# A two-block transformer kernel on one core: residual stream turned to features on partitions, side work spaced by a clock of TensorE time

## The reference, cut to what matters

```
layer A: x += concat(sigmoid(o) * rmsnorm(mlstm(q,k,v,i,f)) * silu(z), memory_attention) @ w_out   # h = rmsnorm(x)
shared:  k, v  = from rmsnorm(x) @ w_kv_a, a latent norm, @ w_kv_b, rmsnorm, rope
layer B: x += concat(chunk_causal_attention(q,k,v) * silu(z), memory_attention) @ w_out
block C: x += (concat(multiscale_pool(u), rms_norm(diff_attention(q,k,v))) * sigmoid(g)) @ w_out
block D: x += memory_cross_attention(rms_norm(x), rms_norm(mem_2)) @ w_co
block E: x += square(relu(rms_norm(x) @ w_up)) @ w_down          # 1024 -> 4096 -> 1024
return rms_norm(x)
```

## Time and profile before

| | |
|---|---|
| median of 3 runs | 1754.74 us (1748.2 to 1758.79) |
| profiled execution, its own time | 1747.94 us |
| span of its trace | 1746.0 us |
| PE matmul busy | 1629.9 us (93% of the span), 7336 records |
| PE weight load busy | 1269.4 us (73%) |
| DVE busy | 889.9 us (51%) |
| ACT busy | 753.1 us (43%) |
| POOL busy | 69.9 us (4%) |
| mean granted TensorE clock | 0.974 |

### The profile page before, as it was taken

One profiled execution on the slowest core, in us unless ns is written; L12 is line 12 of the kernel. 1 busy time (PEld: TensorE's weight loads), 2 busy tenths in 40 slices (PEclk: granted clock), 3 DMA queues, 4 the chain that ended last, 5 costly groups with the idle time before them and its releaser, 6 DMA issues.

```text
span 1746.0 us, 19776 instructions
## 1 busy us (share of the span) xinstructions
PE 1629.9 (93%) x7336; PEld 1269.4 (73%) x7336; DVE 889.9 (51%) x1879; ACT 753.1 (43%) x1714; POOL 69.9 (4%) x64
## 2 busy tenths in 40 slices
PE   6996999999999978899899999889999999999997
PEld 5574777777787866666678877467786878888886
DVE  4367446738445464555544647445444453434343
ACT  6353333324345556666433343335323443434342
POOL 0011001101000000000000000000000000000000
PEclk9998999999999999999999999689999999999999
DMA  6221222222333211111123222013232323333332
GB/s 202 72 82 37 73 61 73 84 62 86 132 103 115 67 38 50 45 46 47 61 74 108 85 73 85 1 50 108 86 108 79 103 85 98 97 100 95 98 98 78
DMA packets 85119, 141.54 MB, mean 81 GB/s; under 512 B 7200, under 2 KB 32160, under 8 KB 85024
## 3 DMA queue, kind: packets, MB, share of 16 engines
q1 hardware_dynamic: 83728, 137.45, 25.5%
q10 hardware_dynamic: 1296, 2.83, 0.5%
HBM read 138.17 MB, written 2.10 MB: 80 GB/s over the span
## 4 chain that ended last, share of the span: by engine, by line
PE 61%; DVE 13%; issue 13%; ACT 10%; DMA 1%; POOL 1%; ACTq 0%; DVEq 0%; SPq 0%; POOLq 0%
PE banks L1059 10%; PE banks L1061 10%; PE banks L1060 10%; PE banks L1054 7%; PE banks L1056 7%; PE banks L1055 7%; DVE sb_arena L1711 3%; ACT sb_junk L1318 3%; PE banks L1019 3%; DVE sb_arena L1720 2%; DVE sb_w_split L1711 2%; ACT sb_w_split L1355 2%; ACT sb_arena L1484 1%; PE banks L1243 1%; DVE sb_arena L1714 1%
## 5 line engine op out<-in xcount | busy, mean ns | idle before, releaser
L1711 DVE TENSOR_TENSOR sb_w_split<-sb_raw,sb_w_split 128x512 fp32r<-128x512 f32 (+4 forms) x520 | 322.6, 662 | 367.2 <-ACT sb_w_split L1355 366.3
L1355 ACT ACTIVATE sb_w_split<-sb_raw 128x512 fp32r<-128x512 f32 (+4 forms) x520 | 286.1, 600 | 352.7 <-PE banks L1061 193.3
L1059 PE MATMUL banks<-sb_w_split,sb_actB 128*128 128x512 f32 (+2 forms) x752 | 302.3, 402 | 7.2 <-DVE sb_w_split L1711 3.0
L1061 PE MATMUL banks<-sb_w_split,sb_actB 128*128 128x512 f32 (+2 forms) x752 | 291.5, 388 | 0.0
L1060 PE MATMUL banks<-sb_w_split,sb_actB 128*128 128x512 f32 (+2 forms) x752 | 291.2, 387 | 0.0
L1054 PE MATMUL banks<-sb_actA,sb_w_split 128*128 128x512 f32 x672 | 271.9, 405 | 1.6 <-DVE sb_arena L1720 1.5
L1056 PE MATMUL banks<-sb_actA,sb_w_split 128*128 128x512 f32 x672 | 262.9, 391 | 0.0
L1055 PE MATMUL banks<-sb_actA,sb_w_split 128*128 128x512 f32 x672 | 262.5, 391 | 0.0
L1059 PE MATMUL banks<-sb_w_split,sb_actA 128*128 128x512 f32 (+1 forms) x416 | 167.8, 403 | 2.2 <-DVE sb_arena L1720 2.2
L1059 PEld LDWEIGHTS banks<-sb_w_split,sb_actB 128*128 128x128 f32 x752 | 144.0, 192 | 32.9 <-DVE sb_w_split L1711 5.6
L1061 PEld LDWEIGHTS banks<-sb_w_split,sb_actB 128*128 128x128 f32 x752 | 143.1, 190 | 28.2
(11 more groups left out here) (163 smaller groups left out, 1864.1 us busy)
## 6 DMA issues: line engine op xcount, KB each, us to landing
sb_raw<-in_a_w_in SPq DMA_DIRECT2D x64, 256.0 KB, 3.0
sb_raw<-in_w_up SPq DMA_DIRECT2D x32, 512.0 KB, 3.6
sb_raw<-in_w_down SPq DMA_DIRECT2D x32, 512.0 KB, 3.7
sb_raw<-in_w_in SPq DMA_DIRECT2D x24, 512.0 KB, 3.6
sb_raw<-in_mem_w_kv SPq DMA_DIRECT2D x16, 512.0 KB, 3.8
sb_raw<-in_a_w_in SPq DMA_DIRECT2D x16, 512.0 KB, 3.7
sb_raw<-in_w_ckv SPq DMA_DIRECT2D x16, 512.0 KB, 3.7
sb_raw<-in_a_w_out SPq DMA_DIRECT2D x12, 512.0 KB, 3.7
```

The costliest lines, as they stand in the source:

```text
L1059: pe.op.matmul(out, x.hi(k)[:, cs], hi, start=i == 0, stop=False)
L1061: t = pe.op.matmul(out, x.lo(k)[:, cs], hi, start=False, stop=last_i)
L1355: act.op.activation(hi[:, cs], raw[:, cs], ACT.Copy).then_inc(act.mark(m("w_hi"), 2 * n + part + 1), 1)
L1711: dve.op.tensor_tensor(out, a, b, op).then_inc(dve.mark(*mark) if mark else dve.tick(), 1)
```

## The change

- **Residual by features.** `x`, `mem` and `mem_2` come in transposed and the result leaves transposed, on the host side of the kernel. `x_res` is [128, 8, 512]. `turn` has no transposes any more: ACT and DVE read `x_res` in SBUF. The products that end in the residual take the form "feature". Squares are written by ACT (`sqa`), added up by POOL (`sqp`), and summed over partitions by PE against a column of ones (`nsq`); the final norm is made in the same way and applied by DVE to eight feature tiles.
- **Planner.** A clock sums the PE time of what is placed (`row_ns`, `side_ns`). A group is taken when the clock has moved by the group's own distance (`lag`) since the last of its lane. `need` now forces only the lane that holds the step (`force`).
- **Layer B reordered**: qlB, ckvB, mk1, mv1, zB0, kvB0, quB0, mqB, kvB1, quB1, mzB0, mzB1 and so on; softmax groups of layer B turn a unit two groups after its scores, with three probability buffers. In D both key products come first, then both query products, then both value products.
- **Gates** by two `tensor_tensor_scan` instructions in place of the eighteen doubling steps.
- **Start**: x is loaded first in eight tiles and `mqA` is the first product, then the memory.

```
-            add(f"{name}{half}", w, nk * P, [(half * 512, 512)], "token", src, "res", order=order, k0=k0)
+            add(f"{name}{half}", w, nk * P, [(half * 512, 512)], "feature", src, "res", order=order, k0=k0)
...
     def advance(self, lane):
-        if self.lanes[lane] and all(a in self.done for a in self.lanes[lane][0][0]):
-            for step in self.lanes[lane].popleft()[1]:
-                self.put_side(lane, step)
+        if self.lanes[lane]:
+            after, steps, lag = self.lanes[lane][0]
+            if all(a in self.done for a in after) and self.clock - self.last[lane] >= lag:
+                self.take(lane)
...
+    def force(self, step):
+
+        if any(step in group for group in self.soon):
+            for s in self.soon.popleft():
+                self.put(s)
+            return
+        lane = next((n for n in (0, 1) if any(step in group[1] for group in self.lanes[n])), None)
+        missing = [a for a in self.lanes[lane][0][0] if a not in self.done]
+        if missing:
+            self.force(missing[0])
+        else:
+            self.take(lane)
...
     def need(self, *steps):
-        tries = 0
-        while not all(s in self.done for s in steps):
-            tries += 1
-            self.step()
+        for step in steps:
+            while step not in self.done:
+                self.force(step)
...
+    def mem_b(h0):
+        rounds(0, [("B", h, i) for h in (h0, h0 + 1) for i in range(TT)], "msc", "mtp", "mval",
+               [("hnscale", "mqB"), ("hnt", "mk1", 3)], [("silu", f"mzB{h0 // 2}", 1)], depth=2, lag=2400)
...
+    latents(0)
+    p.product("mqB")
+    mla(0)
+    head_norm(1, "mqB", TT, True)
+    mem_b(0)
+    mem_b(2)
+    latents(1)
+    p.need(("nrow", "b"))
+    gated("mzB0")
+    gated("mzB1")
+    mla(2)
+    latents(2)
+    p.need(("mval", "B", 3))
+    gated("zB1")
...
-        p.side(0, after, *group)
+        p.side(0, after, *group, lag=4600)
...
+    for kind in ("nsq", "nsum", "ndiag", "nrow"):
+        p.put_side(0, (kind, "f"))
+    for k in range(KD):
+        p.put(("store", k))
...
+            blocks = [(v.sq_sum[norm], 0)] if tiles == TT else [(v.sq_sum[norm], 0), (v.sq_sum[norm], N_MEM)]
+            if norm == "f":
+                blocks += [(v.square_of(norm, n)[1], 0) for n in range(4, KD)]
...
+            for i in range(tiles):
+                for n, (block, at) in enumerate(blocks):
+                    t = pe.op.matmul(v.ps[:, place.bank, i:i + 1], block[:, at + i * P:at + (i + 1) * P], v.con("ones"),
+                                     start=n == 0, stop=n == len(blocks) - 1)
...
         elif kind == "turn":
             name, k = a
-            _, tiles, gain, dst = v.turn(name)
-            second_part(step, dst, k, v.col(gain, k), n=tiles * P)
+            src, gain, dst = v.turn(name, k)
+            dve.wait_ge(*m.at("t_hi", step))
+            fused(dst.lo(k), src, gain, ALU.mult, dst.hi(k).bitcast(F32), ALU.subtract, *m.at("t_lo", step))
...
+            dve.op.tensor_tensor_scan(g[6], g[7], g[5], 0.0, ALU.mult, ALU.add).then_inc(dve.tick(), 1)
...
+            dve.op.tensor_tensor_scan(g[3], g[1], g[1], 0.0, ALU.max, ALU.max).then_inc(dve.tick(), 1)
...
+        elif kind == "sqp":
+            norm, n = a
+            signal, value = m.at("sq_sum", step)
+            pool.wait_ge(*m.at("sq", ("sqa", norm, n)))
+            if n >= 2:
+                pool.wait_ge(signal, value - 1)
+            total = v.sq_sum[norm]
+            pool.op.tensor_tensor(total, total, v.square_of(norm, n)[1], ALU.add).then_inc(signal, 1)
```

More of the change, by code:

```diff
@@ L278, in __init__ @@
         self.chunk_place = []
+        self.clock, self.last = 0.0, [0, 0]
+        self.ahead = 2
     def put(self, step, banks=()):
@@ L358, in product, with after_residual @@
                 self.step()
+    def after_residual(self, name):
+        norm, turn, first = NORM_AFTER[name[:-1]], TURN_AFTER.get(name[:-1]), 4 * int(name[-1])
+        for j in range(first, first + 4):
+            steps = [("turn", turn, j)] if turn else []
+            if first:
+                for step in steps:
+                    self.put(step)
+                self.soon.append(squares(norm, j))
+            else:
+                self.soon.append(steps + squares(norm, j))
     def finish(self):
@@ L371, in order_of_work, with turns, scales @@
     p = Plan()
[L373 to L379 removed]
+    def turns(name, tiles):
+        for k in tiles:
+            p.soon.append([("turn", name, k)])
+    def scales(lane, norm, row=True, after=(), lag=4000):
+        p.side(lane, after, lag=0)
+        p.side(lane, (), ("nsq", norm), ("nsum", norm), lag=lag)
         if row:
[L381 to L383 removed]
+            p.side(lane, (), ("ndiag", norm), ("nrow", norm), lag=4500)
     def head_norm(lane, x, n_tiles, in_softmax):
@@ L397, in head_norm, with rounds @@
                 p.side(lane, (), *steps)
[L399 to L403 removed]
+    def rounds(lane, units, scores, turn_over, values, after, values_after=(), depth=1, lag=4400):
+        complete, first = None, True
+        for n in range(len(units) + depth):
             group = []
@@ L407, in rounds @@
                 complete = None
-            if u is not None:
-                group.append((scores, *u))
-            if before is not None:
-                group.append((turn_over, *before))
-                if before[-1] == TT - 1:
-                    complete = before[:-1]
-            before = u
-            p.side(lane, after if first else values_after if group[0][0] == values else (), *group)
-            first = False
-        p.side(lane, values_after, (values, *complete))
-    turns(0, "memT", range(KD), squares=lambda n: [("sq", "mem", n // 2)] if n % 2 else [])
@@ L421, in order_of_work @@
-    p.side(0, (), ("masks",), ("nsum", "mem"))
-    turns(0, "hA", range(KD), [("load_x", TT - 1)], squares=lambda n: [("sq", "a", n)])
-    scales(0, "a")
-    p.need(("turn", "memT", 3))
-    p.soon.extend([(("load_x", i),) for i in range(2, TT)])
-    p.product("mk0", [("nsum", "mem")])
-    head_norm(1, "mk0", MT, False)
+            if n < len(units):
+                group.append((scores, *units[n]))
+            if n >= depth:
+                u = units[n - depth]
+                group.append((turn_over, *u))
+                if u[-1] == TT - 1:
+                    complete = u[:-1]
@@ new lines, in rounds @@
+            p.side(lane, after if first else values_after if group[0][0] == values else (), *group, lag=lag)
+            first = False
+        p.side(lane, values_after, (values, *complete), lag=1000)
+    for n in range(2):
+        p.put(("load_x", n))
+        p.put(("fetch", n))
+    p.n_fetch = 2
+    p.put(("load_x", 2))
+    p.put(("turn", "hA", 0))
+    p.put(("split", 0))
+    p.put(("fetch", 2))
+    p.put(("load_x", 3))
+    p.put(("turn", "hA", 1))
+    p.put(("split", 1))
+    p.n_split, p.n_fetch = 2, 3
@@ new lines, in order_of_work @@
+    for k in range(4, KD):
+        p.put(("load_x", k))
+        if k % 2:
+            p.put(("fetch", p.n_fetch)) if k == 5 else None
+    p.n_fetch = 4
+    for n in range(4):
+        p.put(("load_mem", n))
+    for k in range(KD):
+        p.soon.append(([("turn", "hA", k)] if k >= 2 else []) + squares("a", k))
+    for n in range(4):
+        p.soon.append([("turn", "memT", 2 * n), ("turn", "memT", 2 * n + 1)] + squares("mem", n))
+    p.soon.append([("masks",)])
+    scales(0, "a", after=[("sqp", "a", 7)], lag=0)
@@ L480, in order_of_work @@
     p.put(("load_again",))
-    turns(1, "memTb", range(KD))
     p.product("outA0")
-    turns(0, "hB", range(4))
+    p.put(("load_mem_again",))
     p.product("outA1")
     p.put(("enter", "outA1"))
-    turns(0, "hK", range(KD))
-    scales(0, "b")
+    turns("hK", range(KD))
+    scales(0, "b", after=[("sqp", "b", 7)])
+    for k in range(KD):
+        p.soon.append([("turn", "memTb", k)])
+    p.product("qlB", [("nsum", "b")])
+    for step in (("qll0",), ("qll1",)):
+        p.side(1, (), step, lag=1500)
```

604 lines of the change are left out of this document (309 added, 295 removed).

## The result

The changed kernel takes 1768.93 us (median of five runs, 1764.55 to 1770.57) beside 1754.74 for the kernel before in the same comparison; the ratio is 1.0078, with a 95% interval of 1.005 to 1.0106: small, but clear of no change. The prediction was 1684, with a range of 1642 to 1716. Its profiled execution has a span of 1768.8 us against 1746.0.

What follows compares the result with a forecast made beforehand. PE was taken as the bound, losing time to side work and waits for late inputs. Terms -27 + 6 - 10 - 22 - 25 - 1 + 0 + 3 + 9 = -67 gave 1684 us, range 1642 to 1716.

Steps and rivals of the forecast that it cites:

- I take 42.3 down to 17: Layer B: longer turn distances remove most waits, about 10 forced memory groups add 11 us back; -25, bounds 0 and -36.
- B not relieved: Rival: layer B's 25 us stays lost through forced groups before zB1 and busier ACT; 1709, chance 0.15.
- Gates: Layer A's gate stretch: scans replace doubling steps and memory softmaxes are no longer forced along; 27.5 to 6, -22 us.
- Both forms stand in that stretch at one pace: Feed-forward blocks: residual products changing from token to feature form keep the same matmul pace; 0 us.
- D: Layer D: m2's squares and additions before nrow m2 at ckD0 make an 8 us stall; 11.0 to 14, +3.
- Start and end: Start: -10, bounds -3 and -15; after the last product matmul: 19.0 us, +9, or +13 with ones at low clock.
- Transposes and ones: PE side matmuls: 240 transposes gone, -27 us; sums against ones for seven norms, +6 us.
- PE's total would be down by some 29: Sign to look for: PE's total busy time down by some 29, 240 transposes at modelled length plus less slow clock.
- C: Layer C: lane still blocked behind gC0, same sixteen softmaxes pile up at outC0; 39.6 stays, 0, bounds -12 and +5.
- The rival of POOL: POOL's 44 additions hold up DVE at each norm; +26 us, 1710, chance 0.06.
- The rival that the kernel gets slower: Distances too long, so needs force groups in bulk in A, B and D; more than 32 extra forced; chance 0.04.

Runs made afterwards that it cites:

- lag0: Kernel after, with the planner taking a group as soon as its conditions hold, whatever its distance: 1775.33 us, 1.0126 of before.
- memfirst: Kernel after, layer B reordered with ckvB first, mqB behind mk1, memory softmaxes before the first pair's attention, pair-turn distances halved: 1765.18 us.
- bonly: Kernel after, only layer B's order changed: mqB, ckvB, mk1, mv1, mzB0, qlB, mzB1, then pairs; pair and latent turn distances 1300: 1753.84 us.
- best3: Kernel after with near, gateblock, bonly's order, mem_2's squares placed in outC1, and dveadd together: 1699.31 us, 0.9706 of before.
- noconv: Kernel after, convolution of head 0 in layer A with two taps instead of four: 1756.49 us, 1.0033 of before.
- gatesfirst: Kernel after, gate matmul groups and the gates' first step put ahead of the norm of mk0 in lane 1: 1782.42 us, 1.0163 of before.
- near: Kernel after, tensor actB allocated right after actA instead of last in SBUF: 1755.58 us, 1.0013 of before.
- gateblock: Kernel after, in block C the group with a head's last dval waits for gC4's gates instead of gC0's: 1738.68 us, 0.9908 of before.
- dveadd: Kernel after, the 44 additions of squares made by DVE instead of POOL: 1761.48 us, 1.0044 of before.
- swap: Kernel after, actA and actB exchanged in the allocation, so actB is second and actA last: 1768.56 us (one run).

## Why the prediction was wrong

**The step that failed most: layer B, 48 us off.** The step was "I take 42.3 down to 17": turns two groups late, distances and two products of room were to take away nearly all of B's waits, and about 10 forced memory groups were to put 11 us back. The planner forces 13 groups, and that stretch loses 17.6: a forced softmax costs more than 2.0 less its own matmuls, because behind short waits the matmuls ran at the low clock. That is 7 of the 48. The rest is the relief that did not come: outside the forced stretch layer B still loses 63, where all of it lost 59.1 before. Forcing 7 groups and not 13 (lag0) changed nothing, so the number forced is not what makes the loss. What was missed is where the side work goes. The new order puts qlB, ckvB, mk1 and mv1 first and mqB eighth, so that the first 97 us (495.7 to 592.5) carry 5 us of side matmuls and all 66 softmax groups come later. I had counted groups against rows from mqB on and never asked what the kernel before did with the rows ahead of it: there mqB came third and the memory softmaxes ran beside ckvB and qlB. With the memory softmaxes early again, memfirst and bonly lose 65.0 and 63.9 instead of 80.8: some 16 of the 48 are the order, the forced stretch included. The other 30 are a relief that no order tried has brought; best3 ends at 59.3, level with the kernel before. The rival "B not relieved" (1709) was the right direction with a floor that was too kind: it let B be as before, not worse.

**Gates, 20 us off (17 with the rest of layer A).** Two assumptions failed. The forecast took all of the loss to be doubling steps and forced softmaxes. The scans alone, in the kernel before, bring 9.7 of 25.3; of the 15.6 that stay, the convolution's DVE work is the one part that a run shows, in the kernel after (noconv, 9.0). And "x first" was costed only at the start: behind it the memory's key norm stands ahead of the gates in their lane, so the gates' matmuls run in qkA0, up to 117.7, and their chain ends after the last row of it, where PE waits 3.27 us for the transposes. gatesfirst shows the price of that, 8.4 us in this stretch. Queue order after a moved load is a part of moving it.

**The operand's place, 11.5 us, absent from the sum.** "Both forms stand in that stretch at one pace" was true of the kernel before and useless, since both operands lay near the front. 144 rows of residual products at 0.08 us each are 11.5, and the 384 matmuls of the token products out of actB add 2.5; near measured 13.4. 5.1 of it (64 rows) more than explain the feed-forward blocks' +4.0, the rest is spread over the other parts of the table and is not to be added to them.

**D, 9 us too small.** The mechanism was right, a chain of squares and additions before `nrow m2` at the foreseen place; its size was not. I put four squares and three additions in it; POOL ran six additions, since those of the residual's own norm stand ahead. With 9.37, 1.81 and 1.03 us idle and the clock at half behind that, 8 us of stall became 17 of loss.

**Start and end.** The first product matmul came at 7.92 us (8.4 predicted). But the stages up to qkA0 lose 3.6 less, not 10, near the bound of 3, though not for its reason: the rows of mqA, now the first product, lose 7.7, and only 0.83 of that is a wait for a split. The longest is for the diagonal of x's own norm, which DVE makes behind evictions and turns of the memory:

```profile
38.03 2.05 PE L1246 MATMUL banks<-sb_arena 128*128 128x512 f32 x2 [3.53 <-DVE sb_arena L1865]
```

The rest is matmuls 0.43 us apart, at half pace, in the first 6 us. The forecast had no term for the norm's chain there. After the last product matmul 21.5 us pass for 19: the twenty ones-matmuls take 6.78 for 4.1, at the low clock, as the bracket of +13 had it.

```profile
1748.75 6.78 PE L1237 MATMUL banks<-sb_cons,sb_arena 128*128 128x1 f32 x40 [1.49 <-issue]
```

**What held.** Transposes and ones: -20.4 by price. That PE's total would be down by some 29 did not hold, since slow matmuls took its place. C: 0 predicted, +2.3; the block behind gC0 is unchanged, and gateblock shows that it is the dearest single line in the kernel after (it stands in the kernel before too, with a pile behind it as well, but was not lifted there). The rival of POOL: dveadd brings 7.4 us of the feared 26, 4.4 of them in D. Beside POOL's additions in D (from 1212.91 on) a pair of splits took 2.56 us, the pair before them 1.29:

```profile
1211.83 1.29 DVE L1862 TENSOR_TENSOR sb_w_split<-sb_raw,sb_w_split 128x512 fp32r<-128x512 f32 x2 [2.33 <-ACT sb_w_split L1505]
1213.90 2.56 DVE L1862 TENSOR_TENSOR sb_w_split<-sb_raw,sb_w_split 128x512 fp32r<-128x512 f32 x2 [0.79 <-ACT sb_w_split L1505]
```

The Trainium skill (SBUF — State Buffer, "SBUF: two separate sides") says that GpSimd and a DVE instruction with two SBUF inputs share a pair of ports, which one of them holds for its whole instruction while the other is blocked. The second row agrees that DVE is held up; the run shows that most of what is held up had slack.

**The forecast's shape.** The rival that the kernel gets slower had 0.04 and came true, but not by its mechanism, bulk forcing by distances: distances were a gain in A and nothing in B (lag0). Each large term was read as what an edit removes. Three of the misses are things that an edit moved: product rows to where no side work was ready, the gates behind another norm, a tensor to the end of memory.

What stays open: which move in layer B's order brings the 16 us, and the last 59 us of layer B, which neither order removes; DVE and ACT alternate there inside each softmax, and no run took that apart.

## What to carry to other kernels

Where one engine sets the pace and the rest is packed around it, an order of products is also a supply of cover: list, for each product, which side work is ready when it runs, before and after, and price the rows that run with none. A wait condition in a queue costs everything behind it; moving one condition in C from the last gate product to the one whose data it guards was worth more than the whole change was meant to bring in any one layer. And an edit of the memory layout is an edit of speed until a trace shows that it isn't.

## What the runs showed of the hardware

- A matmul of 512 columns in fp32r with an operand in the last tensor of SBUF (48 KB, from some 178,000 bytes of the partition on) starts 233.3 ns after the one before it, against 226.7 with the tensor near the front, at the same full clock. It follows the tensor in swap. It holds for the moving operand (dn, up) and for the stationary one (mv0 233.0 and 226.8, kC 233.4 and 228.0). Products out of the memory in the kernel before, whose tensor lies near the front, have 230 to 231, and no run takes that apart. Where between front and end the change comes was not tried.
- At equal work, 7194 matmul records, PE's busy time is 1649.4 us in the kernel after, 1629.5 with one wait condition moved (gateblock) and 1601.2 in best3, of which the place of the operand makes 12.4. In the forced stretch of layer B, waits of 0.4 to 1.5 us, each harmless by itself, are followed by a stretch at 1.2 GHz in which the same value step took 3.75 us instead of 1.96.
- The two scans of 4 x 512 took 1.21 us each; one is shown.

```profile
128.98 1.21 DVE L2051 TENSOR_TENSOR_SCAN sb_arena<-sb_arena 4x512 f32<-4x512 f32 x1
```
